# Three seams of a three-block fp32 kernel: loads moved, keys in two banks, output products inside two attentions

## The reference

```python
mod = c_act @ w_ada[l] + b_ada[l]
shift, scale, gate = jnp.split(mod, 3, axis=-1)
h = rms_norm(x, norm_g[l]) * (1.0 + scale[:, None]) + shift[:, None]
proj = h @ w_in[l]
gq, gk, gv, glr, gz, dq, dk, dv, dz = split_columns(proj)
...
o_gla = gla_branch(gq, gk, gv, glr, gz, w_gk[l], b_gk[l], gla_norm_g[l])
...
o_diff = diff_branch(dq, dk, dv, dz, qn_g[l], kn_g[l], lam, lam_init, diff_norm_g[l])
y = jnp.concatenate([o_gla, o_diff], axis=-1).astype(x.dtype) @ w_out[l]
x = x + gate[:, None] * y
```

## Time and profile before

| | |
|---|---|
| median of 3 runs | 2425.61 us (2424.55 to 2425.86) |
| profiled execution | 2426.89 us |
| its span in the trace | 2424.8 us |
| PE (TensorE) busy | 2329.8 us, 96% |
| DVE (VectorE) busy | 1266.4 us, 52% |
| ACT (ScalarE) busy | 1063.2 us, 44% |
| POOL (GpSimd) busy | 596.5 us, 25% |
| mean granted clock of TensorE | 0.985 |
| DMA | 181.87 MB, mean 75 GB/s |

### The profile page before, as it was taken

The page is one execution under the profiler, slowest core; times in us unless marked ns, Lnnn a source line. Parts: engine busy times, 40 slices in busy tenths (PEclk is TensorE's granted clock), DMA queues, the critical chain, the costliest instruction groups (busy, mean ns, idle before and its releaser), DMA issues. The chain is left out here.

```text
span 2424.8 us, 33122 instructions
## 1 busy us (share of the span) xinstructions
PE 2329.8 (96%) x12824; PEld 1901.2 (78%) x12824; DVE 1266.4 (52%) x1776; ACT 1063.2 (44%) x2258; POOL 596.5 (25%) x411
## 2 busy tenths in 40 slices
PE   6999999889999999999999999998999999999999
PEld 4777787778887777777888887677888888888887
DVE  5855304884644512685551366560687777774121
ACT  4435333673634433575443345553643333334221
POOL 2100020232410021133232121112315444465130
PEclk9999999899999999899999999999999999999999
DMA  7432110104112111003211100003223222246231
GB/s 251 130 126 82 37 53 1 36 1 161 66 44 97 44 52 35 18 19 114 87 61 29 57 1 5 23 10 130 87 70 96 79 87 79 79 145 238 88 137 44
DMA packets 139073, 181.87 MB, mean 75 GB/s; under 512 B 8700, under 2 KB 102307, under 8 KB 138917
## 3 DMA queue, kind: packets, MB, share of 16 engines
q1 hardware_dynamic: 137877, 179.74, 21.7%
q10 hardware_dynamic: 1040, 0.00, 0.0%
HBM read 151.41 MB, written 28.31 MB: 74 GB/s over the span
## 5 line engine op out<-in xcount | busy, mean ns | idle before, releaser
L824 PE MATMUL ps<-w_hi,hT_hi 128*128 128x512 f32 (+1 forms) x384 | 142.2, 370 | 2.1 <-PEq L682 1.0
L824 PE MATMUL ps<-hT_hi,w_hi 128*128 128x512 f32 x360 | 141.2, 392 | 2.8 <-PEq L274 2.8
L824 PE MATMUL ps<-w_lo,hT_hi 128*128 128x512 f32 (+1 forms) x384 | 142.1, 370 | 0.0
L824 PE MATMUL ps<-w_hi,hT_lo 128*128 128x512 f32 (+1 forms) x384 | 142.0, 370 | 0.0
L824 PE MATMUL ps<-hT_lo,w_hi 128*128 128x512 f32 x360 | 140.6, 391 | 0.0
L4012 POOL TENSOR_TENSOR w_lo<-ffn_sums,w_hi 128x512 fp32r<-128x512 f32 x76 | 96.8, 1296 | 171.9 <-ACT w_hi L4194 171.9
L755 POOL TENSOR_TENSOR w_lo<-difp_raw,w_hi 128x2048 fp32r<-128x2048 f32 x8 | 36.8, 4604 | 391.3 <-ACT w_hi L724 391.3
L824 PE MATMUL ps<-hT_hi,w_lo 128*128 128x512 f32 x328 | 128.4, 391 | 0.0
L4062 PE MATMUL ps<-ffn_t_hi,w_hi 128*128 128x512 f32 x304 | 118.4, 389 | 0.7 <-DVE ffn_u L4371 0.7
L4062 PE MATMUL ps<-ffn_t_hi,w_lo 128*128 128x512 f32 x304 | 118.3, 389 | 0.0
L4062 PE MATMUL ps<-ffn_t_lo,w_hi 128*128 128x512 f32 x304 | 118.3, 389 | 0.0
(11 more groups left out here) (575 smaller groups left out, 6509.4 us busy)
## 6 DMA issues: line engine op xcount, KB each, us to landing
ffn_raw<-in_ffn_w_up SPq DMA_DIRECT2D x40, 512.0 KB, 4.7
mix_gla<-in_w_ada SPq DMA_DIRECT2D x32, 512.0 KB, 3.4
ffn_raw<-in_ffn_w_down SPq DMA_DIRECT2D x30, 512.0 KB, 4.6
xres<-big SPq DMA_DIRECT2D x24, 512.0 KB, 2.6
hid<-ffn_f SPq DMA_DIRECT2D x22, 512.0 KB, 2.6
ffn_sums<-hid SPq DMA_DIRECT2D x44, 256.0 KB, 4.0
glap_raw<-in_w_in SPq DMA_DIRECT2D x10, 1024.0 KB, 5.4
difp_raw<-in_w_in SPq DMA_DIRECT2D x10, 1024.0 KB, 5.0
```

What stands on the lines that cost most here:

```text
L824: mm = nc.tensor.matmul(out, l, r, start=(job.part != 1 and c == 0 and k == 0), stop=(job.evac and c == job.chunks - 1 and k == len(pairs) ...
```

## The change

It has four parts.

1. `stage_gla_project`: the parts of the modulation stand two to each of the tiles 0 to 6, and the last two behind the convolutions and the low half of `z`. `stage_gla` begins with the units in banks 2, 3, 0, 1 (`LEADING`) where it follows in the same block, and its wait for the 64 steps is cut into four, one ahead of each group of columns.
2. `keys_and_norm`: the ring has two banks. Step 0's scores (now in banks 2 and 3) stand after tile 3, its maxima and exponentials in tile 4's turn, its combination in tile 5's; the first map of step 1 stands after tile 6, ahead of the last keys, and the second map ahead of the last transposes. Low parts are written one tile earlier. The pairs of banks of the steps are counted backwards.
3. Differential attention: three tiles of the output projection (4, 5, 0) instead of two (0, 1). Tile 4's 12 products stand in four pieces of three in the last three steps and after them; tile 0's in two pieces around the last transposes. The split of tiles 4 and 0 moves into steps 15 and 16, its low half to GpSimd.
4. MLA attention: 36 products of the output projection (tiles 4, 5, 0, second half of the contraction) stand in the last steps, tiles 4 and 5 in pieces of three and six, tile 0 whole at the end. The weights' chunks are loaded second half first, and `stage_out_plain` runs the second half first, without these tiles.

```diff
-OUT_EARLY = 2
+OUT_EARLY = (4, 5, 0)
+PLAIN_EARLY = (4, 5, 0)
...
-    def part_tile(k):
-        return k // 2 if k < 10 else 5 + (k - 10) // 3
+    parts_behind = 2 if mod.early else 0
...
-            for k in range(mod.early):
-                if part_tile(k) == n:
+            for k in (2 * n, 2 * n + 1):
+                if k < mod.early - parts_behind:
                     mod.accumulate(dve, s_mraw(q), q.extra["macc"], k, 0)
...
     def dve_after(dve, q):
+        for k in range(mod.early - parts_behind, mod.early):
+            mod.accumulate(dve, s_mraw(q), q.extra["macc"], k, 0)
         dve.wait_ge(q.extra["gbias"], 16)
...
+    LEADING = (2, 3, 0, 1) if q else (0, 1, 2, 3)
...
-            pe.wait_ge(q.extra["macc"], mod.HALF * mod.early)
-        for u in range(LEAD):
+        for n, u in enumerate(LEADING):
             if q:
                 pe.wait_ge(q.free[u], (q.units - u + NBANK - 1) // NBANK)
             project(u)
             if mod.ahead:
-                mod.columns(pe, U[0], 0, range(u * 2 * KC // LEAD, (u + 1) * 2 * KC // LEAD)).then_inc(s_cols, 1)
+                pe.wait_ge(q.extra["macc"], mod.HALF * mod.early * (n + 1) // LEAD)
+                mod.columns(pe, U[0], 0, range(n * 2 * KC // LEAD, (n + 1) * 2 * KC // LEAD)).then_inc(s_cols, 1)
...
-    G, RING, HALF = DIFF_W // DIFF_DH, 4, KC // 4 * DIFF_W
+    G, RING, HALF = DIFF_W // DIFF_DH, 2, KC // 4 * DIFF_W
...
+            if i == 3:
+                pe.wait_ge(q.free[2], 2)
+                pe.wait_ge(q.free[3], 2)
+                start.products(0, (0, 1)).then_inc(start.s_s, 1)
             if i == NT - 2:
-                pe.wait_ge(s_nk, NT - 2)
-                start.products(0, (0, 1)).then_inc(start.s_s, 1)
-        start.products(1, (0,)).then_inc(start.s_first, 1)
+                pe.wait_ge(s_lo, 2 * (NT - 3))
+                start.products(1, (0,)).then_inc(start.s_first, 1)
+        pe.wait_ge(start.s_p, 2)
+        start.products(1, (1,)).then_inc(start.s_s, 1)
         turn(NT - 1)
...
-        for i in range(NT):
+        for i in range(NT - 1):
+            square(i)
             root(i)
             if i:
                 high(i - 1)
-            if i == NT - 2:
+            if i == 4:
                 for mp in range(2):
                     start.exps(act, 0, mp)
         start.exps(act, 1, 0)
+        square(NT - 1)
+        high(NT - 2)
+        root(NT - 1)
+        start.exps(act, 1, 1)
         high(NT - 1)
...
         for i in range(NT):
+            if i == NT - 1:
+                dve.wait_ge(start.s_first, 1)
+                start.maxima(dve, 1, 0)
...
+            if i == NT - 1:
+                low(NT - 2)
...
-            if 2 <= i < NT - 1:
-                low(i - 2)
-            if i == NT - 2:
-                low(NT - 3)
+            if i == 4:
                 for mp in range(2):
                     start.maxima(dve, 0, mp)
-        low(NT - 2)
-        dve.wait_ge(start.s_first, 1)
-        start.maxima(dve, 1, 0)
+            if i == 5:
+                start.combine(dve, 0)
+            if 1 <= i < NT - 1:
+                low(i - 1)
+        start.maxima(dve, 1, 1)
         low(NT - 1)
...
-            return ps[:, mp, :].rearrange("p (k s) -> p k s", k=4)
-        slot = (2 * n + mp) % 3
+            return ps[:, 2 + mp, :].rearrange("p (k s) -> p k s", k=4)
+        slot = (4 - 2 * n - mp) % 3
...
+    SPLIT = (4, 0, 5, 1, 2, 3, 6, 7)
+    SPLIT_AT = {15: 0, 16: 1}
...
+            def other_half(i, chunks):
+
+                if chunks[0] == 0:
+                    pe.wait_ge(s_p, 2 * n_steps - (2 if i >= 4 else 0))
+                    held.wait_done(pe)
+                    pe.wait_ge(s_olo, SPLIT.index(i) + 1)
+                out_products(nc, m, ps[:, i, :], i, 0, (m.w_hi[:, 0, :], m.w_lo[:, 0, :]), chunks[0] == 0, False, chunks)
+
             for n in range(n_steps + 2):
-                if n + 1 < n_steps:
+                if 1 < n + 1 < n_steps:
                     scores(n + 1)
+                if n >= n_steps - 1:
+                    other_half(4, (n - n_steps + 1,))
...
+            other_half(4, (3,))
             turn_y(NT - 2, n_steps)
-            other_half(0)
+            other_half(5, range(KC // 2))
+            other_half(0, (0, 1))
             turn_y(NT - 1, n_steps)
-            other_half(1)
+            other_half(0, (2, 3))
...
                 held.low(pool, n)
+                if n in SPLIT_AT:
+                    k = SPLIT_AT[n]
+                    toks = slice(P * SPLIT[k], P * SPLIT[k] + P)
+                    pool.wait_ge(s_ohi, k + 1)
+                    pool.tensor_tensor(m.hT_lo[:, 0:4, toks], other[:, :, toks], m.hT_hi[:, 0:4, toks].bitcast(F32),
+                                       ALU.subtract).then_inc(s_olo, 1)
...
-            sp.dma_start(self.raw, self.jobs[n // self.CHUNKS].srcs[0][:, n % self.CHUNKS, :]).then_inc(self.s_raw, 16)
+            sp.dma_start(self.raw, self.jobs[1 - n // self.CHUNKS].srcs[0][:, n % self.CHUNKS, :]).then_inc(self.s_raw, 16)
...
+        def early(tile, chunks):
+            if chunks[0] == 0:
+                pe.wait_ge(s_p, 2 * n_steps - (2 if tile >= 4 else 0))
+            out_products(nc, m, ps[:, tile, :], tile, 1, (m.w_hi[:, 0, :], m.w_lo[:, 0, :]), chunks[0] == 0, False,
+                         chunks)
+
...
             if 1 <= n - 1 < n_steps:
                 turned(n - 1, 0, 0)
+            if n == n_steps - 1:
+                up.mixes_split(pe)
+                held.wait_seconds(pe)
+                early(4, (0,))
+            if n == n_steps:
+                early(5, (0,))
             if n + 1 < n_steps:
                 rope(n + 1)
             if 0 <= n - 1 < n_steps:
                 turned(n - 1, 1, 0)
+            if n == n_steps - 1:
+                early(4, (1, 2))
+            if n == n_steps:
+                early(5, (1,))
             if n >= 2:
                 values(n - 2, 1)
             if 0 <= n - 1 < n_steps:
                 turned(n - 1, 0, 1)
+                if n == n_steps - 1:
+                    early(4, (3,))
+                if n == n_steps:
+                    early(5, (2,))
                 values(n - 1, 0)
                 turned(n - 1, 1, 1)
+                if n == n_steps:
+                    early(5, (3,))
+        early(0, range(KC // 2))
...
-        w = OutWeights(nc, ctx, m, "mixo", jobs, next_jobs)
+        w = OutWeights(nc, ctx, m, "mixo", jobs, next_jobs, (1, 0))
...
-            w.first_columns(pe)
+            w.first_columns(pe, None, PLAIN_EARLY)
```

More of the change, by code:

```diff
@@ L1916, in scores @@
             def scores(n):
[L1917 to L1918 removed]
+                pe.wait_ge(s_p, 2 * n - 1)
+                start.products(n, (0, 1)).then_inc(s_s, 1)
             def turned(n, part):
```

119 lines of the change are left out of this document (61 added, 58 removed).

## The result

The changed kernel takes **2401.28 us** (median of 4 runs, 2399.57 to 2402.48), the kernel before 2425.74 us (also 4 runs): ratio 0.9899, 95% interval 0.9882 to 0.9916. The forecast was 2402. Its profiled execution has a span of 2400.8 us, 24.0 us less than before.

What follows compares the result with a forecast made beforehand. PE, busy 2329.8 of 2424.8 us, bounds the kernel; only waits and half clock can go. 4.5 + 3.6 + 7.8 + 7.8 = 23.7 us gives 2403.2, or 2402 against the runs' median; likeliest 2398 to 2407, with rivals 2394 to 2410.

Steps and rivals of the forecast that it cites:

- seam: Between the first layer's projection and scan: PE's wait for gate-rank copies goes (3.1 us), half clock too (1.4): 4.5 us.
- keys, a layer: From keys to differential attention: step 3's scores start 2.9 us earlier, less 1.1 for step 1's first map: 1.8 us.
- differential tail, a layer: End of differential attention: next stage starts 1.5 us earlier with 2.7 us less to do, less 0.3 cost: 3.9 us.
- MLA tail: End of MLA attention: 8.1 us of products moved in, path 3.1 longer, half clock worth 2.9 gone: 7.8 us.
- The chain: End of the keys: square, reduction, low half and multiplications let the last transposes start 4.4 us after last keys, not 5.7.
- I keep the half clock in this sum: Start of the differential attention: PE still idles 2.2 us between transposes, so half clock stays within the 1.8 us a layer.
- the clock stays full: Rival, start of both differential attentions: full clock since the wait shrinks; 2 x 2.5 us more, 2397 us; chance 0.18.
- 1.5, 2.7 and 0.3: End of differential attention, us a layer: earlier start of next stage, products it no longer does, cost of moved copies and subtractions.
- 1.3 us on the path for each of four: Differential attention: by the exclusion rule alone, moved GpSimd subtractions lie on the path; sum 5 us less, about 2407.
- The seam stayed open: Rival, first layer's seam: another wait, late parts or low weights, replaces the old; 4.5 us not won, 2406.5; chance 0.06.
- the pieces lengthen: Rival, ends of both attention kinds: pieces lengthen what they fill, half of 15.6 us lost, 2410 us; chance 0.13.
- two banks are not short: Against the slower rival, keys: chain over 6.1 us makes PE stand at 12 tiles; 2432 at 2.5 us each; chance 0.03.

Runs made afterwards that it cites:

- e1: Changed kernel with the first layer's seam as before (unit order, single wait, placement of the modulation's parts): 2405.77 us, ratio 0.9910.
- e2: Changed kernel with the keys and queries stage as before (four banks, steps 0 and 1 placed as before): 2405.76 us, ratio 0.9912.
- e3: Changed kernel with the end of the differential attention as before (tiles 0 and 1, no pieces, splits behind the loops): 2412.39 us, ratio 0.9933.
- e4: Changed kernel with the end of the MLA attention as before (no output products in it, old order of weight halves): 2410.48 us, ratio 0.9931.
- e8: Changed kernel plus six products nobody reads, ahead of the scores of the MLA attention's tile 0: 2401.53 us, ratio 0.9902.
- e11: Changed kernel with tile 4's twelve products in one piece behind the differential attention's last values, instead of four pieces: 2405.53 us, ratio 0.9914.
- e9: Changed kernel without tile 0's twelve products at the end of the MLA attention, pieces of tiles 4 and 5 kept: 2406.02 us, ratio 0.9914.
- e10: Changed kernel without the eight pieces of tiles 4 and 5 in the MLA attention, tile 0's products kept: 2407.18 us, ratio 0.9921.
- e5: Changed kernel with only the order of the first scan units as before (0, 1, 2, 3): 2402.46 us, ratio 0.9898.

## Why the prediction was right, point by point

| term | forecast | measured | by |
|---|---|---|---|
| seam | 4.5 | 4.72: wait 3.3, clock 1.4; 3.78 where the old seam had no slow stretch | before, e1 |
| keys, a layer | 1.8 | 2.5; 1.2 to 1.8 with equal slow time | before, e2, e3, e4, e8, twenty passages |
| differential tail, a layer | 3.9 | 3.74 | e3 |
| MLA tail | 7.8 | 7.5; 5.97 in the profiled pair | e4 |
| sum | 23.7 | 24.7 (4.7 + 5.0 + 7.5 + 7.5) | 24.46 by medians, 24.0 by spans |

**Seam.** The steps came as forecast: convolution, weight subtraction, copies, no wait, late parts done at 154.52 (155.2 forecast). Both halves were sized about right. From the projection's last product to the first scan unit it was 3.52 us and is 0.23, so the wait is worth 3.3 (3.1 forecast); from there to the next projection 130.2 and 128.8, so the clock is worth 1.4, as forecast. That the clock's part counts is partly luck: e1 ran the old seam at full clock, and there undoing it cost 3.78 us, of which nearly all is a wait that had come out 0.4 us longer.

**Keys.** The chain held: the last transposes start 4.35 us after the last keys end (4.4 forecast). Step 3's scores start 9.7 and 10.0 us after the last keys end, 11.35 forecast at the half clock; where it did lie there, in e3, they start at 10.5. The step that failed is "I keep the half clock in this sum": in layer 0 it began only with these scores and lasted 3.4 us, and over all passages it was 3.4 to 13.7 us long behind the last keys. So the case "the clock stays full" at 2397 came true by a part, which no experiment could turn into a rule. Two more terms were off and made up for each other. With equal slow time (13.7 us: e2's layer 1, e8's layer 0) step 3's scores are won 3.8 us early and 2.7 are left at the first output, where 2.9 stood. And the keys take 1.5 us longer, where 1.1 stood for the first map of step 1: in the changed kernel the products of tiles 5, 6 and 7 start at 401.91, 408.27 and 416.03, so that tile 7 comes 1.4 us later behind tile 6 than tile 6 behind tile 5, the price of that map's 7 products. The ring itself costs nothing: its trace has no wait of PE for a bank of keys.

**Differential tail.** The next stage starts 86.14 us after the first output's transposes instead of 87.15 and has 2.7 us of products less to do. Without the 0.2 us of the moved splits that is 1.2 us of waits, against 1.5, 2.7 and 0.3. The term that was too large is the waits: pieces cover 0.61 us each, not 0.68 (e11).
On GpSimd against VectorE the trace decides. By the rule of the Trainium skill ("SBUF — State Buffer", Who interferes with whom) such a subtraction and a combination exclude each other while one of them runs. The prediction's estimate from this, 1.3 us on the path for each of four, took 5 us off the sum. Measured are 0.4 us in all: all four subtractions fell into gaps between combinations. The rule isn't refuted, it had nothing to act on.

**MLA tail.** The path grew by 3.36 us (1637.53 to 1652.14 before, 1620.96 to 1638.93 now; 3.1 forecast), the boundary's wait fell from 3.01 to 0.30, and the half clock there is gone in all traces that keep the part whole. 8.1 less 3.4 is 4.7 where 5.0 stood (8.1 less 3.1); by e9 and e10 tile 0 is worth 2.3 us and the pieces 1.9, or 3.4 with the slow stretch of e10. The rest of the 7.5, 2.8 us, goes with the clock, 17.1 against 10.2 us at half, as forecast (2.9). The prediction saw the half clock only behind the boundary; in e4 half of it lies in the last steps. In the profiled pair 1.5 us of it hid behind one slow stretch more at 1507.

**The rivals.** The seam stayed open in no form; the pieces lengthen only in the MLA attention, within the sum; two banks are not short.

**The number.** That 2402 lies within 1 us of the median is in part luck. The keys gave 1.4 us more in the two layers than forecast, mostly by the clock, the other terms together 0.4 less, and executions of one kernel lie several us apart.

## What to carry to other kernels

A wait at a hand-written seam is fixed where the late engine's queue is too full, and the reader's order is the cheap second half: moving two parts that nobody needs yet behind the convolutions won 3.1 of 3.8 us (e5). Independent products of a later stage were worth nearly their full time in a bare wait (e9: all of 2.7 us but 0.4; e11: 90%), and about a third of it where they also lengthen the path (e10: 1.9 of 5.4, if its extra slow stretch is chance). Price such edits by distances between landmarks that both kernels have, and compare stretches with equal time at half clock: here these repeat to 0.1 or 0.2 us where medians are uncertain by 4 to 6.

## What the runs showed of the hardware that was not expected

The same instructions, undisturbed by an edit, ran with different amounts of half clock from one execution to the next, in stretches of 3.4, 6.8, 10.2, 13.7 or 17.1 us. Between the projection behind layer 1 and the MLA attention's first transposes, it took 281.4 us in six executions, that of before among them, and 279.8 in the eight others: the window of the changed kernel at 1326.0 is at 0.50, that of e1 at the same place within 0.5 us, 1327.2, at 1.00.

```profile
1326.00:1329.40 3.40, 3.40 (x10) 2.63 (x9) 0.53 (x4) 2.02 (x7) 0.00 (x0) 0.50 0.78 229
```

```profile
1327.20:1330.60 3.40, 3.38 (x15) 2.83 (x16) 0.58 (x4) 2.46 (x7) 0.00 (x0) 1.00 0.67 182
```

3.4 us at half cost 1.5 to 1.6 us where PE is busy, and there are a handful of such places. That is enough for differences of several us between executions of one kernel, and the mean clocks on record go with them: the runs of e1 took 2401.02 and 2402.82 us at 0.995 and 0.994, 2408.72 and 2409.16 at 0.989 and 0.988. Where the half clock lay, only the profiled executions show. The work of PE right before does not decide it: 3.4 us with 0.02 us of work at e1's seam were not followed by half clock, while in the changed kernel 1.20 us of 3.4 before 431.70 were, and 3.4 of 3.4 before 1506.90. What decides it was not found.
